# A two-layer hybrid trunk on one core: attention's first pairs inside the projections, a reordered last head step, six-chunk loads

## The chip, the core and the metric

The kernel runs on 1 core of one Trainium2 chip. The metric is the device time of one execution in microseconds (us), as the median of 3 runs. Engines are named as the profile names them: PE (TensorE), DVE (VectorE), ACT (ScalarE), POOL (GpSimd), SP (SyncE, which issues the loads).

## The reference, cut to what matters

Two layers run over 256 context and 512 latent tokens of width 1024, in float32. Layer 0 mixes tokens with a bidirectional gated recurrence (8 heads of 128), layer 1 with windowed attention. Each is followed by a feed-forward block with a 3x3 depthwise convolution. All of it is modulated by rows made from `c` and `ada_w`.

```python
def gla_chunk_step(state, q, v, k, g):            # layer 0, one chunk, both directions
    b = jnp.cumsum(g, axis=-2)
    o_inter = einsum(q * jnp.exp(b), state)
    o_intra = einsum(einsum(q, k, decay), v)
    state = jnp.exp(b_end)[..., :, None] * state + einsum(k * jnp.exp(b_end - b), v)
...
def sink_attend(q, keys, vals, sink, mask):       # layer 1, per block of 128 queries
    logits = where(mask, einsum('bqgrd,bkgd->bgrqk', q, keys) * 64 ** -0.5, -inf)
    m = maximum(max(logits, axis=-1), sink)
    p = exp(logits - m[..., None])
    o = einsum('bgrqk,bkgd->bqgrd', p / (sum(p, axis=-1) + exp(sink - m)), vals)
...
def conv_ffn(h, w_up, conv_w, conv_b, w_down, on_grid):
    u, v = split(h @ w_up)
    return (gelu(conv3x3(u) + conv_b) * v) @ w_down
```

## The kernel before, in words

**Matrix products.** Every activation and weight is split into a high and a low part (`HH`/`HL`, `WH`/`WL`), and each product is three matmuls. A weight tile is 8 chunks of 128x128 (512 KB). SP loads it into `WR[t % 3]` once tile t-3 is done (L387), ACT makes `WH` from it (`split_high`, L1106), DVE makes `WL` in the place of `WR` (`split_low`, L1555), and PE waits for that (`begin_tile`). ACT and DVE do this up to two tiles ahead of the tile that they follow, at fixed places of their instruction order. `depth(t)` says how many chunks are loaded and split: 6 for the eight tiles of the first output projection, 8 for all others. The third group of each feed-forward block has only 6 chunks of rows (`GROUPS = (8, 8, 6)`), so the last two chunks of its eight down tiles are zeros that PE never multiplies.

**The recurrence.** Each of the 8 heads has a step: seven levels of scores on PE (`level_scores`), between which DVE merges keys, queries and totals and takes the scores out of `MA` (`take`). PE does the next head's projections in between. The states of head h are made during the step of head h+1: PE turns the keys (`key_value`, L679), ACT copies them, PE multiplies them with the values (L687), DVE adds the states up (`states`, L1830 and L1832), and PE makes the outputs (`outputs`, L696). `key_value` waits for the final keys of the head (`kq_final`), for the modulation row (`ada_ready`, L1594), and for the scores to be taken (`scores_read`) before it writes `MA`. In steps 0 to 6 half a projection tile stands ahead of `key_value` on PE. In the last step (`last_head_step`) there is no projection left, PE begins with `key_value`, and fills the gaps with units of the output projection (`out_units`), one chunk of one tile each. Such a unit needs the low part of a finished head, which POOL makes (L409, `early_lo`) from ACT's high part.

**Attention.** Twelve tiles of projections come first (tiles `T_AT` to `T_AT + 11`), in two halves of key, four queries and value. DVE rotates keys and queries, ACT rounds them (L1459). Then 32 pairs of units (two heads, one block of 128 queries each) go round: PE makes a pair's scores into `MB` and `MA` (L933), DVE masks them and takes the maximum into `PB` (`masked_max`, L2159), ACT takes the exponential (`at_exp`, L1495), DVE inverts the sum (L2167), POOL scales (L440), PE turns the probabilities into `SLOT[0]` (L943), ACT copies them (L1509), and every four pairs PE multiplies with the values (L966). There is one `MB` and one `MA`: the scores of pair k wait for the maxima of pair k-1 (`row_max`). Scores run `LEAD = 2` pairs ahead of the turns. There are 7 buffers `PB`. The first three lie where the end of `HL` is (read until the last projection), the last four where the raw modulation weights were.

Of the kernel before, what the change touches and what calls it, by code (L numbers as in the profile page):

```python
# [27 lines left out]
P = 128  # L28
# [53 lines left out]

def depth(t):

    return EARLY if T_HGO <= t < T_HGO + KC else KC


# [23 lines left out]
def trunk(nc, small_in, x_in, ada_in, w_in, ident_in, masks_in, rope_in, rot_in, tri_in, out):  # L111
    ctx = ExitStack()
    with ctx:
# [3 lines left out]
        def sem(name):  # L117
            return ctx.enter_context(nc.semaphore(name))
# [13 lines left out]
        WH = [sb(f"WH{i}", [P, KC, P], F32R) for i in range(NB)]  # L132
        with ExitStack() as s:
            rope = sb("rope", [P, 2, LAT], F32, s)
            PB += [sb(f"PB{i}", [P, 5 * P + 1], F32, s) for i in range(3, 7)]
        AR0 = sb("ada_raw", [P, 4, 2, 512])
        AR = [AR0[:, i, :, :] for i in range(4)]
        ident = sb("ident", [P, P])
# [106 lines left out]
        level_ready, scores_done, scores_read = sem("level_ready"), sem("scores_done"), sem("scores_read")  # L245
        keys_ready, keys_mixed = sem("keys_ready"), sem("keys_mixed")
        v_turned, v_ready = sem("v_turned"), sem("v_ready")
        kq_final, k_turned, kt_ready = sem("kq_final"), sem("k_turned"), sem("kt_ready")
        kv_done, states_ready = sem("kv_done"), sem("states_ready")
        early_hi, early_lo = sem("early_hi"), sem("early_lo")  # L250
# [93 lines left out]
        def _(sp):  # L344
# [26 lines left out]
            def weights(t):  # L371

                if T_AT < t < T_AT + 6:
                    return w_in[T_AT - 2 + AT_ORDER[t - T_AT]]
                if T_FF0 < t < T_FF0 + 3:
                    return w_in[T_FF0 - 2 + (2 if t == T_FF0 + 1 else 1)]
                if t < T_HGO:
                    return w_in[t]
                if t < T_HGO + KC:
                    return w_in[t, :, 0:EARLY, :]  # L380
                if t < T_FF0:
                    return w_in[T_HGO:T_HGO + KC, :, t - KC - T_HGO + EARLY, :].rearrange("n p o -> p n o")
                return w_in[t - 2]

            for t in range(NB, STEPS):
                sp.wait_ge(tile_done, t - NB + 1)
# [16 lines left out]
        @block.gpsimd  # L403
        def _(pool):
            def split_heads():

                for h in range(HEADS - 1):
                    pool.wait_ge(early_hi, h + 1)
                    pool.tensor_tensor(HL[:, h, :], Y[:, h, :], HH[:, h, :].bitcast(F32), ALU.subtract).then_inc(early_lo, 1)  # L409

            def weights_low(t):

                pool.wait_ge(w_hi_done, t + 1)
                pool.wait_ge(w_split, t)
                pool.tensor_tensor(WL[t % NB][:, :, :], WR[t % NB][:, :, :], WH[t % NB][:, :, :].bitcast(F32), ALU.subtract).then_inc(w_split, 1)

            weights_low(0)
            split_heads()
            for t in POOL_LOWS:
                weights_low(t)  # L420

            def sink_columns():

                pool.wait_ge(nsink_ready, 1)
                for u in range(len(UNITS)):
                    i, bi, r, part = UNITS[u]
                    hd, n = i * 8 + part * 4 + r, chunks(u)
                    if u >= NPB:
                        pool.wait_ge(p_turned, u - NPB + 1)
                    pool.tensor_scalar(PB[u % NPB][:, n * P:n * P + 1], nsink[:, hd:hd + 1], 1.0, 0.0, ALU.mult, ALU.add).then_inc(sink_col, 1)  # L430
                    if u >= 3:
                        scaled_probs(u - 3)
                for u in range(len(UNITS) - 3, len(UNITS)):
                    scaled_probs(u)

            def scaled_probs(u):

                n = chunks(u) * P
                pool.wait_ge(rden_ready, u + 1)
                pool.tensor_scalar(PB[u % NPB][:, 0:n], PB[u % NPB][:, 0:n], rden[u % 4][:, :], 1.0, ALU.mult, ALU.mult).then_inc(probs_scaled, 1)  # L440

            pool.wait_ge(tile_done, T_AT + 12)
            sink_columns()

        @block.tensor
        def _(pe):
# [309 lines left out]
            def last_head_step(b):  # L756
# [4 lines left out]
                level_scores(b, -1)  # L761
                out_units(2)
                head_sums()
                level_scores(b, 0)
                out_units(7)
                level_scores(b, 1)
# [141 lines left out]
            def at_projections():  # L908

                first_tiles(TOK)  # L910
                third_tile(LAT)
                value_turns(MB, 1)
                for j in range(3):
                    full_tile((j + 1) % 2, LAT, HH, HL)
                full_tile(0, TOK, HH, HL)
                for j in range(4):
                    full_tile((j + 1) % 2, LAT, HH, HL)
                full_tile(1, TOK, HH, HL)

            def at_scores_of(k):  # L920

# [83 lines left out]
            def attention():  # L1005

                at_scores_of(0)
                pe.wait_ge(evacuated[0], tile.half(1))
                pe.wait_ge(evacuated[1], tile.half())
                value_turns(SLOT[0])  # L1010
                at_scores_of(1)
                pe.wait_ge(v_ready, vals.now(-2))
                for k in range(PAIRS):
                    if k + LEAD < PAIRS:
                        at_scores_of(k + LEAD)
                    at_turn(2 * k)
                    at_turn(2 * k + 1)
                    if k >= 4:
                        v, n = k // 4 - 1, chunks(8 * (k // 4 - 1))
                        cs = ((0, 1), (2, 3), (4,), ())[k % 4][:max(0, n - 2 * (k % 4))]  # L1020
# [73 lines left out]
        def _(act):  # L1094
# [377 lines left out]
            def projected(i):  # L1472
# [8 lines left out]
                for j in range(1, 5):  # L1481
                    raw((j + 1 - i) % 2, i * 6 + j)
                    rounded(i, j - 1)
                    if i == 0 and j == 1:
                        value_copy_at(0, MB)
                if i == 1:
                    new_values(i)
                rounded(i, 4)

            def at_exp(u):  # L1490

# [18 lines left out]

            def attention():

                at_exp(0)
                at_exp(1)
                value_copy_at(1, SLOT[0])
                for u in range(2, 2 * LEAD):
                    at_exp(u)
                for k in range(PAIRS):
                    at_copy(2 * k)
                    at_copy(2 * k + 1)  # L1520
                    for u in range(2 * k + 2 * LEAD, min(2 * k + 2 * LEAD + 2, len(UNITS))):
                        at_exp(u)
                    if k in EARLY_OUT:
# [14 lines left out]
        def _(dve):  # L1538
# [312 lines left out]
            def head_step(b, parity, h, j0, tail=True, project=True):  # L1851
# [12 lines left out]
                for n in range(LEVELS):  # L1864
                    merge_keys(b, n)
                    if tail and n == 0:
                        head_out(h - 1)
                    merge_queries(b, n, taken.now() + 1)
                    take(n)
                    merge_totals(b, n)  # L1870
                    if project and n in (0, 2, 3, 4):
                        split_low(first + (3 if n == 0 else n + 2))
                rows.add()
                ada_add(j0)
                if project:
                    gate(parity, h + 1)

# [8 lines left out]
            def last_head_step(b, j0):  # L1886

                forget(b, 0, 7)
                decayed_queries(b)
                states(1 - b)  # L1890
                diagonal(b)
                head.add()
                take(LEVELS)
                split_low(T_HGO + 2)
# [235 lines left out]
            def projected(i):  # L2130
# [7 lines left out]
                rope_low(5 * i)  # L2138
                for j in range(1, 5):
                    rope_sums(5 * i + j)  # L2140
                    split_low(first + j + 3)
                    rope_low(5 * i + j)
                tile.add(6)
# [44 lines left out]

            def attention():

                for u in range(2 * LEAD):
                    masked_max(u)
                    if u >= 2:
                        inverse_sum(u - 2)
                for k in range(PAIRS):
                    for u in range(2 * k + 2 * LEAD, min(2 * k + 2 * LEAD + 2, len(UNITS))):
                        masked_max(u)
# [124 lines left out]
```

## Time and profile before

| | us |
|---|---|
| median of 3 runs | 1839.48 (1839.29 to 1841.08) |
| the profiled execution's own time | 1840.51 |
| its span in the profile | 1838.4 |
| PE busy | 1795.9 (98%) |
| DVE busy | 1163.5 (63%) |
| ACT busy | 680.5 (37%) |
| POOL busy | 79.3 (4%) |
| head steps and first projections, 60 to 600: PE busy of 540.0 | 532.9 |
| attention pairs, 1289 to 1403: PE busy of 114.0 | 103.2 |
| end of the last feed-forward and final norm, 1784 to 1838.4: PE busy of 54.4 | 44.2 |

The profiled execution's own time is its span and 2.1 us around it. Its rows give times from the start of the span. The granted PE clock is given as a share of 2.4 GHz: 1.00 is full speed and 0.50 is 1.2 GHz.

### The profile page before, as it was taken

Reading aid. Unit: us, or ns where it says so; the run is one execution under the profiler, and the core shown is the slowest. Engines: PE = TensorE matmul, PEld = TensorE weight load, DVE = VectorE, ACT = ScalarE, POOL = GpSimd, SP = SyncE. Lnnn points to the kernel's source line nnn. Section 1 sums busy time; section 2 is a strip of 40 time slices with the busy share of each in tenths; the row PEclk is TensorE's granted clock in tenths of the full one; section 3 lists DMA queues with packets and bytes.
Section 4 is the critical chain, followed back from the end, with each engine's and each line's share of the span. In section 5 each row is a group of like instructions: output and inputs, shape, how many; then the busy total and the mean of one; then the engine's idle time right before and its main releaser. Section 6 shows DMA issues by size and latency. Waiting matters only on the chain.

```text
span 1838.4 us, 31654 instructions
## 1 busy us (share of the span) xinstructions
PE 1795.9 (98%) x13574; PEld 1535.3 (84%) x13574; DVE 1163.5 (63%) x1934; ACT 680.5 (37%) x1009; POOL 79.3 (4%) x142
## 2 busy tenths in 40 slices
PE   8999999999999999999999999999899999999997
PEld 7999999999888788888888888888556888888886
DVE  5366668666887776425653356477555697487585
ACT  4334434443432433213331132343775343243233
POOL 0000000000110100000000000000453000000000
PEclk9999999999999999999999999999999999999998
DMA  9321222112211233223323232222000232232233
GB/s 307 106 102 41 88 93 93 67 65 90 85 45 35 81 115 115 94 108 120 115 92 104 104 123 92 84 71 83 12 1 24 69 106 100 93 99 96 92 102 105
DMA packets 54154, 166.18 MB, mean 90 GB/s; under 512 B 5120, under 2 KB 15744, under 8 KB 54016
## 3 DMA queue, kind: packets, MB, share of 16 engines
q1 hardware_dynamic: 54016, 164.16, 26.0%
q8 instruction: 108, 1.77, 0.4%
q14 instruction: 30, 0.25, 0.0%
HBM read 162.05 MB, written 2.10 MB: 89 GB/s over the span
## 4 chain that ended last, share of the span: by engine, by line
PE 91%; DVE 5%; ACT 2%; issue 1%; DMA 1%; POOL 0%; DVEq 0%; SPq 0%; ACTq 0%
PE slot L478 31%; PE slot L466 8%; PE slot L468 7%; PE slot L467 7%; PE slot L1051 4%; PE slot L1053 4%; PE slot L1052 4%; PE MA L662 2%; PE MB L535 2%; PE MA L1051 2%; PE MA L1053 2%; PE MA L1052 2%; PE slot L966 2%; PE MB L933 1%; PE slot L943 1%
## 5 line engine op out<-in xcount | busy, mean ns | idle before, releaser
L1555 DVE TENSOR_TENSOR WL<-WR,WH 128x1024 fp32r<-128x1024 f32 (+1 forms) x203 | 246.0, 1212 | 206.4 <-ACT WH L1106 204.8
L1106 ACT ACTIVATE WH<-WR 128x1024 fp32r<-128x1024 f32 (+1 forms) x206 | 215.9, 1048 | 381.1 <-DMA WR<-in_w 381.1
L466 PE MATMUL slot<-HH,WH 128*128 128x384 f32 (+2 forms) x768 | 270.7, 353 | 9.7 <-DVE HL L1656 5.0
L468 PE MATMUL slot<-HH,WL 128*128 128x384 f32 (+2 forms) x768 | 261.6, 341 | 0.0
L467 PE MATMUL slot<-HL,WH 128*128 128x384 f32 (+2 forms) x768 | 261.5, 340 | 0.0
L478 PE MATMUL slot<-HH,WH 128*128 128x256 f32 (+1 forms) x768 | 201.9, 345 | 0.3 <-DVE WL L1555 0.3
L478 PE MATMUL slot<-HH,WL 128*128 128x256 f32 (+1 forms) x768 | 198.5, 340 | 0.0
L478 PE MATMUL slot<-HL,WH 128*128 128x256 f32 (+1 forms) x768 | 196.0, 337 | 0.0
L466 PEld LDWEIGHTS slot<-HH,WH 128*128 128x128 f32 x768 | 145.0, 189 | 23.8 <-DVE HL L1656 6.0
L478 PEld LDWEIGHTS slot<-HH,WH 128*128 128x128 f32 x768 | 141.5, 189 | 23.9 <-issue 5.7
L478 PEld LDWEIGHTS slot<-HL,WH 128*128 128x128 f32 x768 | 145.0, 189 | 17.1
L478 PEld LDWEIGHTS slot<-HH,WL 128*128 128x128 f32 x768 | 144.7, 188 | 16.5
L468 PEld LDWEIGHTS slot<-HH,WL 128*128 128x128 f32 x768 | 144.7, 188 | 4.1
L467 PEld LDWEIGHTS slot<-HL,WH 128*128 128x128 f32 x768 | 144.9, 189 | 3.2
L2064 DVE SCALAR_TENSOR_TENSOR ACC<-UP,cw,ACC 128x512 f32<-128x512 f32 x176 | 132.0, 750 | 20.9 <-ACT ACC L1413 17.7
L1992 DVE SCALAR_TENSOR_TENSOR ACC<-UP,cw,ACC 128x512 f32<-128x512 f32 x176 | 131.9, 750 | 3.9
L1051 PE MATMUL slot<-HH,WH 128*128 128x512 f32 x256 | 99.9, 390 | 0.0
L1052 PE MATMUL slot<-HL,WH 128*128 128x512 f32 x256 | 99.6, 389 | 0.0
L1053 PE MATMUL slot<-HH,WL 128*128 128x512 f32 x256 | 99.6, 389 | 0.0
L478 PE MATMUL slot<-GH,WH 128*128 128x256 f32 (+1 forms) x308 | 79.0, 338 | 0.0
L478 PE MATMUL slot<-GL,WH 128*128 128x256 f32 (+1 forms) x308 | 78.4, 336 | 0.0
L478 PE MATMUL slot<-GH,WL 128*128 128x256 f32 (+1 forms) x308 | 78.4, 335 | 0.0
(297 smaller groups left out, 3167.7 us busy)
## 6 DMA issues: line engine op xcount, KB each, us to landing
WR<-in_w SPq DMA_DIRECT2D x198, 512.0 KB, 3.5
ada_raw<-in_ada SPq DMA_DIRECT2D x84, 512.0 KB, 4.5
AD<-in_ada SPq DMA_DIRECT2D x12, 512.0 KB, 8.5
X<-in_x SPq DMA_DIRECT2D x4, 768.0 KB, 9.1
WR<-in_w SPq DMA_DIRECT2D x8, 384.0 KB, 3.0
out<-Y SPq DMA_DIRECT2D x8, 256.0 KB, 2.2
Y<-in_masks SPq DMA_DIRECT2D x1, 512.0 KB, 8.8
rope<-in_rope SPq DMA_DIRECT2D x1, 512.0 KB, 3.8
```

The lines of the kernel that those rows point to most:

```text
L466: mm(SLOT[s][:, po], WH[w % NB][:, k, :], hi[:, k, to], start=(k == 0), stop=False)
L467: mm(SLOT[s][:, po], WH[w % NB][:, k, :], lo[:, k, to], start=False, stop=False)
L468: last = mm(SLOT[s][:, po], WL[w % NB][:, k, :], hi[:, k, to], start=False, stop=(k == kn - 1))
L478: last = mm(dst[:, po], wt[w % NB][:, k, :], x[:, k, to], start=(k == 0 and part == 0), stop=(k == kn - 1 and part == 2))
L535: last = mm(MB[32 * m:32 * m + 32, 0:P], silu_w[:, c, :], src(f)[:, m * P:(m + 1) * P], start=(c == 0), stop=(c == KC - 1))
L1051: mm(dst, WH[w % NB][:, k, :], hi[:, k, t], start=(k == 0), stop=False)
L1052: mm(dst, WH[w % NB][:, k, :], lo[:, k, t], start=False, stop=False)
L1053: last = mm(dst, WL[w % NB][:, k, :], hi[:, k, t], start=False, stop=(k == kn - 1))
L1106: go(WH[t % NB][:, 0:depth(t), :], WR[t % NB][:, 0:depth(t), :], ACT.Copy).then_inc(w_hi_done, 1)
L1555: tt(WL[t % NB][:, 0:k, :], WR[t % NB][:, 0:k, :], WH[t % NB][:, 0:k, :].bitcast(F32), ALU.subtract).then_inc(w_split, 1)
L1992: ins = stt(acc, lat[:, dy:dy + GRID_H, dx:dx + GRID_W], cw[b][:, k:k + 1], acc, ALU.mult, ALU.add)
L2064: ins = stt(acc, grid[:, dy:dy + GRID_H, dx:dx + GRID_W], cw[b][:, k:k + 1], acc, ALU.mult, ALU.add)
```

## The change

It has three parts.

1. **Attention's first pairs.** The four `PB` buffers in the modulation weights' place now come first in the ring. PE makes the scores of pair 0 ahead of the last projection tile, those of pair 1 inside it (after 5 of its 8 chunks), and those of pair 2 right behind it. The maxima, exponentials and the first inverse sum of units 0 to 3 move into the projections' code on DVE and ACT, between the rotation and rounding of the last query and the copy of the last values. POOL starts its sink columns once tile `T_AT + 6` is done, and waits for the last tile ahead of unit 4. The turn of the last values on PE moves behind the turns of units 0 and 1, and goes to `SLOT[1]`.
2. **Head steps.** In every head step but the last, DVE adds the modulation row ahead of the last `take` and the last totals, and no longer behind them. In the last head's step DVE makes the states and the diagonal first and the decayed queries behind them; a new semaphore `queries_ready` holds PE's `level_scores(b, 0)` until then.
3. **Six chunks.** `depth(t)` is 6 for the last eight tiles of both feed-forward blocks, for the load and both splits.

```diff
 def depth(t):
 
+    if T_AT - KC <= t < T_AT or t >= STEPS - KC:
+        return GROUPS[-1]
     return EARLY if T_HGO <= t < T_HGO + KC else KC
...
-            PB += [sb(f"PB{i}", [P, 5 * P + 1], F32, s) for i in range(3, 7)]
+            PB = [sb(f"PB{i}", [P, 5 * P + 1], F32, s) for i in range(3, 7)] + PB
...
-                return w_in[t - 2]
+                return w_in[t - 2, :, 0:depth(t), :]
...
+                    if u == 2 * LEAD:
+                        pool.wait_ge(tile_done, T_AT + 12)
...
-            pool.wait_ge(tile_done, T_AT + 12)
+            pool.wait_ge(tile_done, T_AT + 7)
             sink_columns()
...
                 head_sums()
+                pe.wait_ge(queries_ready, 1)
                 level_scores(b, 0)
...
-                full_tile(1, TOK, HH, HL)
+
+            def at_last_tile():
+
+                begin_tile(1)
+                for k in range(KC):
+                    both_halves(1, k, HH, HL)
+                    if k == 4:
+                        at_scores_of(1)
...
                 at_scores_of(0)
+                at_last_tile()
+                at_scores_of(LEAD)
                 pe.wait_ge(evacuated[0], tile.half(1))
-                pe.wait_ge(evacuated[1], tile.half())
-                value_turns(SLOT[0])
-                at_scores_of(1)
-                pe.wait_ge(v_ready, vals.now(-2))
                 for k in range(PAIRS):
-                    if k + LEAD < PAIRS:
+                    if 0 < k < PAIRS - LEAD:
                         at_scores_of(k + LEAD)
                     at_turn(2 * k)
                     at_turn(2 * k + 1)
+                    if k == 0:
+                        pe.wait_ge(evacuated[1], tile.half())
+                        value_turns(SLOT[1])
+                    if k == 3:
+                        pe.wait_ge(v_ready, vals.now(-2))
...
                     rounded(i, j - 1)
+                    if i == 1 and j == 4:
+                        at_exp(0)
+                        at_exp(1)
+                        rounded(i, 4)
+                        at_exp(2)
+                        at_exp(3)
...
                 if i == 1:
                     new_values(i)
-                rounded(i, 4)
+                else:
+                    rounded(i, 4)
...
-                at_exp(0)
-                at_exp(1)
-                value_copy_at(1, SLOT[0])
-                for u in range(2, 2 * LEAD):
-                    at_exp(u)
                 for k in range(PAIRS):
                     at_copy(2 * k)
                     at_copy(2 * k + 1)
+                    if k == 0:
+                        value_copy_at(1, SLOT[1])
...
                     merge_queries(b, n, taken.now() + 1)
+                    if n == LEVELS - 1:
+                        rows.add()
+                        ada_add(j0)
                     take(n)
...
-                rows.add()
-                ada_add(j0)
...
                 forget(b, 0, 7)
-                decayed_queries(b)
                 states(1 - b)
                 diagonal(b)
+                tt(QQ[b][:, :, :], Q[:, :].unsqueeze(1).to_broadcast([P, 2, TOK]), FD[b][:, :, :], ALU.mult).then_inc(queries_ready, 1)
...
                     rope_sums(5 * i + j)
+                    if i == 1 and j == 4:
+                        masked_max(0)
+                        masked_max(1)
+                        inverse_sum(0)
+                        rope_low(5 * i + j)
+                        masked_max(2)
+                        inverse_sum(1)
+                        masked_max(3)
+                        split_low(first + j + 3)
+                        continue
                     split_low(first + j + 3)
                     rope_low(5 * i + j)
...
-                for u in range(2 * LEAD):
-                    masked_max(u)
-                    if u >= 2:
-                        inverse_sum(u - 2)
```

## Rows read from the trace of the kernel before

**Rows 1.** Waits of PE, 1500:1838: us in total, times, longest.

```profile
PE slot L1051 <- DVE WL L1555: 1.0, 1, 1.0
...
PE slot L1051 <- DVE GL L2039: 0.5, 1, 0.5
```

**Rows 2.** Chain that ended last, the last projection tile: start, us.

```profile
1280.76 8.49 PE slot L478 x48
```

**Rows 3.** PE timeline, start of attention: start us, us, [idle before <-releaser].

```profile
1289.16 0.38 PE L933 MATMUL MB<-KH,QH 64*128 64x256 f32 x1
...
1290.32 0.85 PE L905 MATMUL slot<-ident,AVT 128*128 128x128 f32 x6 [0.17 <-ACT AVT L1470]
1292.90 0.35 PE L933 MATMUL MB<-KH,QH 64*128 64x256 f32 x1 [1.74 <-DVE nmax L2159]
...
1295.56 0.55 PE L933 MATMUL MB<-KH,QH 64*128 64x256 f32 x1 [1.68 <-DVE nmax L2159]
...
1298.84 0.38 PE L933 MATMUL MB<-KH,QH 64*128 64x256 f32 x1
```

**Rows 4.** DVE timeline, last tile and start of attention.

```profile
1284.76 0.69 DVE L2121 TENSOR_TENSOR RAW<-RAW,ROT 128x512 f32<-128x512 f32 x1
...
1291.33 0.74 DVE L2159 CUSTOM_DVE_ANT_0 PB<-MB,edge,nsink 128x512 f32<-128x512 f32 x1
```

**Rows 5.** ACT timeline, the same stretch.

```profile
1289.27 0.90 ACT L1470 ACTIVATE AVT<-slot,small 128x768 f32<-128x768 f32 x1 [3.95 <-PE slot L478]
...
1292.12 0.72 ACT L1495 ACTIVATE PB<-PB,nmax 128x513 f32<-128x513 f32 x1
```

**Rows 6.** PE timeline, into the last head's step.

```profile
495.20 0.33 PE L528 MATMUL MB<-ident,RB 128*128 128x128 f32 x1
499.20 0.90 PE L679 MATMUL MB<-ident,KK 128*128 128x128 f32 x6 [3.68 <-issue]
...
508.60 0.38 PE L696 MATMUL MB<-PS,V 128*128 128x128 f32 x2
...
515.16 0.27 PE L662 MATMUL MA<-QQ,KL 128*32 128x32 f32 x4
```

**Rows 7.** DVE timeline, into the last head's step.

```profile
496.26 1.04 DVE L1817 COPY_PREDICATED PS<-masks,MA 128x384 f32<-128x384 uint8 x2
497.20 1.83 DVE L1805 TENSOR_TENSOR FD<-FD 128x6 f32<-128x6 f32 x2
498.95 0.15 DVE L1594 TENSOR_TENSOR ada<-MB,small 128x8 f32<-128x8 f32 x1
...
501.56 1.76 DVE L1764 TENSOR_TENSOR QQ<-Q,FD 128x1536 f32<-128x1536 f32 x1
504.57 0.29 DVE L1830 COPY SF<-MB 128x128 f32<-128x128 f32 x1 [1.25 <-PE MB L687]
...
508.04 1.39 DVE L1769 TENSOR_TENSOR KL<-KK 128x768 f32<-128x768 f32 x1
```

**Rows 8.** POOL timeline, the same stretch.

```profile
497.11 3.60 POOL L409 TENSOR_TENSOR HL<-Y,HH 128x768 fp32r<-128x768 f32 x2 [471.97 <-ACT HH L1237]
```

**Rows 9.** One stretch: us, busy us and count of PE, PEld, DVE, ACT, POOL, clock, DMA.

```profile
500.00:503.00 3.00, 3.00 (x13) 2.81 (x12) 2.97 (x2) 2.39 (x4) 0.71 (x1) 0.50 0.02 7
```

**Rows 10.** The page's DMA issues: count, KB each, us to landing.

```profile
WR<-in_w SPq DMA_DIRECT2D x198, 512.0 KB, 3.5
...
WR<-in_w SPq DMA_DIRECT2D x8, 384.0 KB, 3.0
```

**Rows 11.** Groups by shape, weight splits, DVE then ACT: count | busy us, mean ns.

```profile
L1555 DVE TENSOR_TENSOR WL<-WR,WH 128x1024 fp32r<-128x1024 f32 x195 | 238.4, 1223 | 205.1 <-ACT WH L1106 203.5 <-DVE KO L2135 0.3
...
L1555 DVE TENSOR_TENSOR WL<-WR,WH 128x768 fp32r<-128x768 f32 x8 | 7.6, 952 | 1.3 <-ACT WH L1106 1.3
...
L1106 ACT ACTIVATE WH<-WR 128x1024 fp32r<-128x1024 f32 x198 | 209.2, 1057 | 375.3 <-DMA WR<-in_w 375.3
...
L1106 ACT ACTIVATE WH<-WR 128x768 fp32r<-128x768 f32 x8 | 6.7, 836 | 5.9 <-DMA WR<-in_w 5.9
```

More of the change, by code:

```diff
@@ L247, in trunk @@
         v_turned, v_ready = sem("v_turned"), sem("v_ready")
+        queries_ready = sem("queries_ready")
         kq_final, k_turned, kt_ready = sem("kq_final"), sem("k_turned"), sem("kt_ready")
```

## The prediction

> **What bounds the kernel now.** I read the page first: PE is busy 98% of the span, so time can only come out of PE's idle gaps or its slow clock. The list of PE's waits says where the gaps are, the timelines of each gap say which chain ends it. Three gaps matter here. At the start of attention PE stops for 1.74 us and 1.68 us, each time for a maximum from DVE, and the next scores run at half clock (0.55 us for the form that takes 0.38 us before and after) [rows 3]. At the start of the last head's step it stops for 3.68 us [rows 6], and then runs 3.0 us at clock 0.50 [rows 9]. In the last feed-forward it stops for 0.5 us for a `GL` chunk and for 1.0 us for a `WL` tile [rows 1]. The reader is to see in each what the awaited engine was doing just before: it was doing other work, or its chain started late.
>
> **Attention's start.** PE's order before is last tile, scores 0, value turns, scores 1, scores 2, turns of pair 0, scores 3. The last tile runs 1280.76 to 1289.16, 8.40 us [rows 2, 3]; scores of a pair take 0.95 us (1289.16 to 1290.15, where the 0.17 us wait before the turns begins) [rows 3]. A pair's maxima hold the next scores for 1.57 us from DVE's first maximum (1291.33 to 1292.90) [rows 3, 4].
>
> Afterwards, step by step. Scores 0 put the last tile at 1281.7. Its fifth chunk ends 5/8 of 8.40 later, 1286.95. DVE ends the last query's rotation at 1285.45 [rows 4], so the maxima of pair 0 start at 1285.4 and release PE at 1287.0, which costs 0.05. Scores 1 end at 1287.95, the tile's other three chunks (3.15) at T = 1291.1. On ACT an exponential starts 0.79 after its maximum (1291.33 to 1292.12) and takes 0.72 [rows 4, 5]: units 0 and 1 run from 1286.2 to 1287.6. The last rounding and DVE's low part behind it are passes over 512 columns as long as the rotation's (0.69) [rows 4], less overlap 1.3 together: 1288.9. The maxima of units 2 and 3 start there and release PE at about 1288.9 + 1.65 = 1290.55 (1.57 and a small inverse between), ahead of T. So scores 2 follow the tile without a gap and end at 1292.05.
>
> What is late next is ACT. Its fourth exponential ends at 1291.15; then comes `WH` of tile T_AT+13 (1.06) [rows 11], which before was hidden inside the last tile, and only then the copy of the last values (0.90) [rows 5], ready at 1293.0. DVE's `split_low` of that tile waits for it from 1290.4 to 1292.25 and takes 1.15 net, and the maxima of units 4 and 5 are queued behind it: 1293.4, PE released at 1293.4 + 1.57 = 1295.0. Meanwhile PE turns units 0 and 1 and the values: 8 and 6 turns, six of which take 0.85 [rows 3], so about 2.0 us, to 1294.1. POOL's scaling of unit 1 is held until T and lies under scores 2; uncovered, it would eat into the 0.9 us that PE then stops for the maxima anyway. So scores 3 start at 1295.0 where they started at 1298.84 [rows 3]: **3.85 us**. From there the order, the buffers and the lead of two pairs are those of before, each pair again held by the one `MB` and `MA`, so the 3.85 stay. The moved matmuls are the same in number; the removed gaps are 3.6 and the lost half clock about 1.1, less a new gap of about 0.9. Bounds: 4.8 if DVE's stop for the `WH` copy (0.9 of PE's time) costs nothing, 2.0 if ACT's block is late by two exponentials and a copy more and PE stops at T for it.
>
> **The last head's step.** PE has its row turned at 495.53 and then needs the add. DVE does it at 498.95, behind a `take` (from 496.26) and the totals (1.83 us for two operations on 6 columns) [rows 6, 7]. The queries' merge before the `take` is over at 496.26. With the add there (0.15), `ada_ready` comes at 496.4 and `key_value` starts at 496.55 in place of 499.20: 2.65 us. Its `MA` half waits for the `take` (1.04), which then ends at 497.45: six turns (0.65) behind 496.55, PE stops for 0.25. The first unit of the output projection needs POOL's first low part, which ends at 497.11 + 1.81 (half of 3.60) = 498.95, PE would be there at 497.45 + 0.65 = 498.1: with the signal's way, 0.95 lost [rows 8]. Between 499.20 and 508.60 PE had no other gap, and 3.0 us of that were at half clock, worth 1.5 [rows 6, 9]. With the gap cut from 3.68 to 1.0 I take it that the clock holds: outputs could start at 508.60 - 2.65 + 0.25 + 0.95 - 1.5 = 505.65. The states must be there. DVE's sequence up to the forget product ends at 501.56 as before (the add only changed places, `take` and totals are still in it). The states took 3.47 (504.57 to 508.04) [rows 7]; ahead of the queries they run from 501.6, when the first products arrive, to 505.1. With the queries' product (1.76) still in front they would end at 506.9 and cost PE 1.25. So outputs start at 505.65 against 508.60: **2.95 us**. Bounds: 1.45 if the clock falls again, 3.5 if PE doesn't meet the two short waits' full lengths.
>
> The product then runs behind the diagonal. Queued behind it on DVE are the first `take` and the split of tile T_HGO+2. Its reader is `level_scores(b, 0)`, 6.55 us behind the start of outputs (508.60 to 515.16) [rows 6]: 512.2. Diagonal and product cost 1.39 and 1.76 [rows 7] behind 505.1, so 508.25, a cover of 3.95 us; POOL has four other low parts to make, 1.8 each [rows 8], and each of the two may stand behind one of them, so at the latest 511.9, still covered. In steps 0 to 5 PE has half a projection tile ahead of `key_value`, and shows no stop there: the earlier add is worth nothing.
>
> Here a rule bears on the move. DVE's totals, both inputs in SBUF, took 1.83 for 6 columns and ended at 499.03, just as POOL's first low part was over (498.9) [rows 7, 8]. The Trainium skill (SBUF — State Buffer, the practical consequences of the shared port pair) says that a DVE instruction with two SBUF inputs and a GpSimd instruction that reads SBUF exclude each other, the second waiting until the first has finished. By that rule the queries' product, which ran alone before, can be held by POOL for whole operations. The trace agrees in that one place. By rule or by row, the sum stays, because of the cover above; the case where the hold is longer than the cover is a rival below.
>
> **Six chunks.** `WH` falls from 1.06 to 0.84, `WL` from 1.22 to 0.95 [rows 11], a load from 3.5 to 3.0 [rows 10]. The first gap (0.5) ends a chain of ACT and DVE work that has one `WH` and one `WL` of a down tile in it: 0.22 + 0.27 = 0.49 off, the gap is gone. The second (1.0) is the fourth down tile, loaded only when the first is done: load, `WH` and `WL` in series, 0.5 + 0.22 + 0.27 = 0.99 off, gone too. **1.45 us**. In layer 0's block PE waits nowhere in these tiles, so nothing there. Bounds: 0.5 (the load lands no earlier) to 1.5 (both gaps are all there is).
>
> **Sum.** 3.85 + 2.95 + 1.45 = 8.25. The profiled execution took 1840.51 (span 1838.4 and 2.1 around it), so 1832.25; the median lies 1.03 below that execution, so 1831.2, 0.45% less.
>
> **Rivals.**
> - *The clock falls again in the last head's step.* For it: in about 3.5 us PE still stops for 1.0, 0.25 and 0.95, and at attention's start it fell with no gap above 1.74 [rows 3]. Against: the longest gap is a third of before. The step gives 1.45, time 1832.7. Chance 0.2.
> - *ACT's block is late.* Exponentials, rounding, `WH` and value copy in one queue delay the first pairs' turns; attention gives 2.0, time 1833.1. Chance 0.13.
> - *The queries' product is held by POOL beyond its cover.* At 511.9 plus the first `take` (1.04) PE waits 0.7, and one POOL operation more makes it 2.5: time 1833.7. Chance 0.07.
> - *The six chunks do nothing*, since ACT's table load and not the load decides when `WH` starts: 1832.2 to 1832.7, inside the range. Chance 0.08.
> - *Slower: PE stays at half clock in attention's pairs.* Scores, turns and short stops alternate there, and it did fall for three microseconds at their start. A microsecond of work at 2.4 GHz costs one more at 1.2, so from 8.25 us of work more at the low clock the gain is gone, and from 12 on it is over 0.2% slower. With 20, the time is about 1843. Against it: the gaps get fewer, and the same pairs kept full speed before. Chance 0.03.
>
> **How the numbers follow.** The forecast has 0.49. A measurement of this kernel can tell about 0.2% (3.7 us) from no change, so faster means below 1835.8. The rivals above zero gain reach 1833.7 one at a time, two together 1835; the best case (4.8 + 3.5 + 1.5) gives 1829.7. The range 1829.0 to 1835.0 leaves out the slow side, three rivals together and gains beyond all three bounds: under 2 in 10. Faster 0.92, same 0.05, slower 0.03.
>
> **What would show it.** Right: the last tile with scores 1 inside and no stop over 0.2 us; scores 2 right behind it; a stop near 0.9 ahead of scores 3 that is DVE's maximum; L1594 ahead of the last `take`; the stop before L679 near 1.0 and none before L696; no wait for `WL` or `GL` at the end. Wrong: a stop in the middle of the last tile, a clock of 0.50 in the last head's step or over a long stretch of attention, a new wait at L662 for `QQ`, or pair cycles that are longer than before.

## The result, and the profile of the changed kernel

The changed kernel takes 1829.49 us (median, 1828.4 to 1830.8) where the kernel before took 1839.51 beside it: ratio 0.9942, 95% interval 0.9928 to 0.9955. It is faster by 10.0 us by the medians and 10.7 by the ratio, where 8.25 was forecast. The forecast time was 1831.2, with a range down to 1829.0: the median of 1829.49 lies at that end of it, and the ratio applied to 1839.48 gives 1828.8, past it. The same file measured again on another chip gave 1831.47 and 0.9955 (0.9942 to 0.9967), 8.1 to 8.3 us. Two single executions of the experiments at a far lower granted clock, 2331 us of the kernel before (0.70) and 2508 us of the one with six chunks alone (0.65), are left out of the ratios.

The profiled execution took 1828.88 us, its span is 1826.7 against 1838.4. To place the 11.7 us between the spans, I measured the distance from one landmark on PE to the next in both traces. The start of the kernel, which no line of the change touches, is 1.60 shorter. The last head's step is 3.04 shorter (forecast 2.95), the stretch from the norm ahead of attention's projections to the fifth scores 4.00 (forecast 3.85; counted from the end of the last query tile alone it is 4.05), the end of the last feed-forward 1.27 (forecast 1.45). What is left is 0.24 in the norms and first feed-forward, 0.60 in the norm behind attention and 0.95 around the final norm. So the three parts sum to 8.31 where 8.25 was forecast, and 3.4 us come from places that the prediction didn't count. The other head steps, in which the add also moved, took the same: 341.45 and 341.46 us from the first head's sums to the last head's row turn, as forecast.

**Attention's start.** PE's timeline; it answers to [rows 3].

```profile
1275.79 0.38 PE L946 MATMUL MB<-KH,QH 64*128 64x256 f32 x1
...
1282.11 0.38 PE L946 MATMUL MB<-KH,QH 64*128 64x256 f32 x1
...
1286.34 0.38 PE L946 MATMUL MB<-KH,QH 64*128 64x256 f32 x1
...
1287.25 1.09 PE L956 MATMUL slot<-ident,PB 128*128 128x128 f32 x8
1288.18 0.82 PE L911 MATMUL slot<-ident,AVT 128*128 128x128 f32 x6
1289.97 0.35 PE L946 MATMUL MB<-KH,QH 64*128 64x256 f32 x1 [0.98 <-DVE nmax L2190]
...
1292.57 0.35 PE L946 MATMUL MB<-KH,QH 64*128 64x256 f32 x1 [0.34 <-DVE nmax L2190]
```

These are the first matmuls of scores 0 to 4, with two groups of turns ahead of scores 3. Scores 0, 1 and 2 have no bracket (a bracket is idle time of the engine, and what ended it): the two stops of 1.74 and 1.68 us are gone, and each scores' first matmul takes 0.38, so the clock is full. One new stop of 0.98 stands ahead of scores 3. What ends it is seen on ACT, then on DVE, in the same stretch:

```profile
1286.19 1.04 ACT L1122 ACTIVATE WH<-WR 128x1024 fp32r<-128x1024 f32 x1
1287.13 0.88 ACT L1486 ACTIVATE AVT<-slot,small 128x768 f32<-128x768 f32 x1
```

```profile
1287.26 1.23 DVE L1575 TENSOR_TENSOR WL<-WR,WH 128x1024 fp32r<-128x1024 f32 x1 [1.83 <-ACT WH L1122]
1288.40 0.74 DVE L2190 CUSTOM_DVE_ANT_0 PB<-MB,edge,nsink 128x512 f32<-128x512 f32 x1
```

DVE is idle for 1.83 us until ACT's `WH` copy, makes `WL`, and only then starts the maximum of unit 4, whose data had been there since 1287.2. This is the chain that the prediction named.

**The last head's step.** PE's timeline, which answers to [rows 6], and one stretch of it with its clock, which answers to [rows 9].

```profile
493.62 0.33 PE L533 MATMUL MB<-ident,RB 128*128 128x128 f32 x1
494.94 0.85 PE L684 MATMUL MB<-ident,KK 128*128 128x128 f32 x6 [0.99 <-DVE QQ L1810]
495.87 0.87 PE L684 MATMUL MA<-ident,KK 128*128 128x128 f32 x6
497.50 0.59 PE L483 MATMUL slot<-HH,WH 128*128 128x256 f32 x2 [0.76 <-POOL HL L412]
...
503.98 0.38 PE L701 MATMUL MB<-PS,V 128*128 128x128 f32 x2
...
510.51 0.27 PE L667 MATMUL MA<-QQ,KL 128*32 128x32 f32 x4
```

```profile
500.00:503.00 3.00, 3.00 (x23) 2.75 (x22) 2.66 (x10) 1.25 (x2) 3.00 (x2) 1.00 0.00 0
```

The stop of 3.68 is now 0.99, the clock stays at 1.00, and the outputs (L701) start 10.36 us behind the row turn (L533) instead of 13.40 (508.60 less 495.20). DVE in the same stretch, which answers to [rows 7]:

```profile
494.68 0.16 DVE L1614 TENSOR_TENSOR ada<-MB,small 128x8 f32<-128x8 f32 x1
494.75 1.05 DVE L1837 COPY_PREDICATED PS<-masks,MA 128x384 f32<-128x384 uint8 x2
495.70 1.76 DVE L1825 TENSOR_TENSOR FD<-FD 128x6 f32<-128x6 f32 x2
...
503.57 2.52 DVE L1789 TENSOR_TENSOR KL<-KK 128x768 f32<-128x768 f32 x1
506.02 3.36 DVE L1912 TENSOR_TENSOR QQ<-Q,FD 128x1536 f32<-128x1536 f32 x1
```

The queries' product took 3.36 where it took 1.76 alone, and the diagonal in front of it 2.52. The product ends at 509.38 and the `take` behind it at 510.35; PE comes for both at 510.51, without a stop, 0.16 to spare.

**The end.** PE's waits from 1500 on; they answer to [rows 1]:

```profile
PE MB L604 <- DVE rstd L1635: 0.6, 1, 0.6
PE slot L1067 <- DVE WL L1575: 0.2, 1, 0.2
```

Of the 1.5 us of stops in the down tiles 0.2 is left (0.5 in the second profile of this kernel). The wait for `rstd` is in the final norm, and is 0.6 in the kernel before too.

### The profile page after: what moved, and what is told of

It reads as the page before. It is cut to its first block, busy times and chain, and to the rows that moved or that the text cites. A ratio compares the mean times of both kernels' runs of the same rounds, so it can differ in the third digit from the quotient of the medians.

```text
span 1826.7 us, 31654 instructions
## 1 busy us (share of the span) xinstructions
PE 1791.4 (98%) x13574; PEld 1531.4 (84%) x13574; DVE 1160.4 (64%) x1934; ACT 677.0 (37%) x1009; POOL 81.0 (4%) x142
## 4 chain that ended last, share of the span: by engine, by line
PE 90%; DVE 6%; ACT 2%; issue 1%; DMA 1%; POOL 0%; DVEq 0%; SPq 0%
PE slot L483 30%; PE slot L471 8%; PE slot L473 7%; PE slot L472 7%; PE slot L1067 4%; PE slot L1069 4%; PE slot L1068 4%; PE MA L667 2%; PE MB L540 2%; PE MA L1069 2%; PE MA L1067 2%; PE MA L1068 2%; PE slot L979 2%; PE MB L946 1%; PE slot L956 1%
## 5 line engine op out<-in xcount | busy, mean ns | idle before, releaser
L1575 DVE TENSOR_TENSOR WL<-WR,WH 128x1024 fp32r<-128x1024 f32 (+1 forms) x203 | 241.8, 1192 | 202.8 <-ACT WH L1122 201.5
```

What stands on the lines that cost most here:

```text
L1575: tt(WL[t % NB][:, 0:k, :], WR[t % NB][:, 0:k, :], WH[t % NB][:, 0:k, :].bitcast(F32), ALU.subtract).then_inc(w_split, 1)
```

## The experiments

Ratios are to the kernel before, run on the same chip. "Outputs" is the distance from the last row turn to the first matmul of the outputs; by it a run's luck at the start drops out. Each run has one profiled execution. Two theories were to be told apart. The first: the three parts give what the prediction's sum says, and the rest of the 10.0 us is the spread of single runs. The second: one part brings more than it was priced at.

**The kernel before once more**

> The kernel before once more, unchanged, for a second profile of it. The changed kernel's profiled span is 11.7 us shorter, of which the three changed places hold 3.90 (attention's start), 2.99 (last head's step) and 1.28 (last down tiles), 8.17 together; the other 3.5 lie where no line was changed: 1.6 before 130 us, 0.4 around the first feed-forward's norm, 0.6 at the norm behind attention and 0.9 at the final norm. Theory 1, these are one run's luck (when the first loads land, and whether PE's clock is at half there): the second profile of before shows other values in these places, by up to 2 us in sum, and the same values in the changed places within 0.1. Theory 2, they belong to the kernel before: the second profile shows the same clock of 0.50 behind 1828 and 0.66 from 1455 to 1460, and a time within 0.3 us of 1839.5.

1840.35 us, span 1838.2. Neither theory held whole. Of the places without changed lines, the norm behind attention moved as luck would have it: 6.77 us from its first sum to the next product where the first profile has 8.47, and no low clock there; the start didn't move. But a changed place moved too, by 0.8 and not within 0.1: outputs came 14.21 us behind the row turn, not 13.40. The clock in the stretch was low for 6.8 us, not 3.4.

**Each part alone**

First attention's part (the last tile with scores 1 inside, the scores, maxima and exponentials moved, POOL's earlier start), then the head steps' part, then the loads:

```
 def depth(t):
+    if T_AT - KC <= t < T_AT or t >= STEPS - KC:
+        return GROUPS[-1]
...
-                return w_in[t - 2]
+                return w_in[t - 2, :, 0:depth(t), :]
```

> Attention's part alone. Theory 1 (the places add up, each with its own size): 3.9 us less than before, ratio 0.9979, plus up to 1.5 if the norm behind attention keeps its clock. Theory 2 (the parts help one another through PE's clock): about a third of the 10 us, but not 3.9. In the trace scores 3 start 3.9 us sooner than in before, counted from the end of the last query tile; the half clock at scores 2 is gone.

> The head steps' part alone. Theory 1: 3.0 us less than before, ratio 0.9984. In the trace the outputs start 10.4 us behind the turned row (13.4 in before), with stops of 1.0 and 0.8 us ahead of them. Theory 2: the earlier phase changes the clock at the first norm as well, up to 1 us more.

> The six-chunk part alone. Theory 1: 1.3 to 1.5 us less than before, ratio 0.9992, all of it in the last eight tiles, none in layer 0. Theory 2: PE's clock at the final norm fell because of the two stops of 0.5 and 1.0 us ahead of it; then the clock behind 1826 stays full as well and the part is worth 2.2 us.

| part alone | us | ratio (95%) | gain in us, from the ratio |
|---|---|---|---|
| attention's start | 1836.81 | 0.9977 (0.9968 to 0.9986) | 4.2 |
| last head's step | 1837.50 | 0.9979 (0.9969 to 0.9988) | 3.9 |
| six chunks | 1837.85 | 0.9986 (0.9977 to 0.9995) | 2.6 |

Each interval is about 1.7 us to either side, so the sum, 10.7, is good to some 3 us (the three added as independent errors). The traces are finer. From the end of the last query tile to the fifth scores attention's kernel took 16.77 us, and the changed kernel 16.78 and 16.77 in its two profiles. The nine profiles in which this place is as before fall into two groups: 20.8 to 21.0 in five of them, both of the kernel before among these, and 21.7 in four, where the clock was low for 6.8 us and not 3.4. One of the four is the kernel with the states' move alone, below:

```profile
1292.00:1298.00 6.00, 4.32 (x30) 3.58 (x27) 3.13 (x12) 3.18 (x8) 1.77 (x5) 0.50 0.00 0
```

So this part gives 4.05 to 4.9 us. In the head's kernel outputs came at 10.37, with the stops 0.99 and 0.75. In the kernel with six chunks all waits for `WL` and `GL` were gone; its outputs came at 14.16, again later than 13.40. The measured sum agrees with the whole gain, and of the two theories the second has the head's step and attention's start on its side: both are priced against an execution with a short stretch of low clock, and often it is longer.

**The changed kernel again, and two mended versions**

The second kernel puts ACT's `WH` copy ahead of the third exponential; the third one also gives PE its `key_value` whole, ahead of the first projection unit.

```
                         at_exp(1)
+                        split_high(tile.now() + AHEAD)
                         rounded(i, 4)
...
-                key_value(1 - b, 1)
-                out_units(3)
+                key_value(1 - b)
+                out_units(4)
```

> The changed kernel once more, unchanged, beside the same runs of before as the next ones. Before itself spread over 1836.2 to 1845.1 in 26 runs. Theory 1 (the changed places give 8.2 by the one profile, and a little more on average since before's half clock in the last head's step was 3.0 us long in its first profile and 5 to 6 us in three others): 8.9 to 9.5 us less than before, ratio 0.995. Theory 2 (a further gain somewhere else): 10 us or more, ratio at or below 0.9945, and a stretch without changed lines that is shorter than in all profiles of before.

> The changed kernel with ACT's high part of weight tile T_AT+13 moved ahead of the exponentials of units 2 and 3, where ACT stood idle for 1.43 us. Theory 1 (the stop of 0.98 ahead of scores 3 is DVE waiting for that copy, with the maxima of units 4 and 5 queued behind it): the stop goes, scores 3 start 0.9 to 1.0 sooner, and so does all that follows; 0.9 us less than the changed kernel. Theory 2 (the exponentials are late by it, or POOL's scaling is next): the stop shrinks by less than 0.5, the time is the same.

> As the one before, and in the last head's step PE multiplies keys and values ahead of the first output unit and makes four units behind them in place of one and three. Theory 1 (PE's stop of 0.76 is POOL's first low part; the key copies of ACT are ready sooner): the outputs start 0.3 to 0.5 sooner than in the changed kernel, so 1.3 us less than it in all. Theory 2 (then the states end the wait): a stop of 0.3 to 0.5 ahead of the outputs takes its place and nothing is won.

The changed kernel: 1831.47, ratio 0.9955, 8.1 to 8.3 us and so less than the 8.9 to 9.5 that I expected. With the early `WH`: 1830.47, 0.9948 (0.9935 to 0.9960). With both: 1830.05, 0.9949 (0.9935 to 0.9962). The times can't tell the three apart, but the traces do. With the early `WH` the stop ahead of scores 3 is gone and scores 3 start 13.14 us behind scores 0 (1278.11 there), not 14.18:

```profile
1291.25 0.37 PE L946 MATMUL MB<-KH,QH 64*128 64x256 f32 x1
```

This shows that the copy's place was what made the stop. With `key_value` whole outputs came at 10.06, as PE now waits for 0.20 in place of 0.76:

```profile
495.15 0.85 PE L684 MATMUL MB<-ident,KK 128*128 128x128 f32 x6 [0.99 <-DVE QQ L1811]
497.15 1.38 PE L692 MATMUL MB<-V,RF 128*128 128x128 f32 x10 [0.20 <-ACT RF L1243]
```

**The early add alone, and the states' move alone**

The early add is in the kernel before, with the product still in front of the states:

```
+                    if n == LEVELS - 1:
+                        rows.add()
+                        ada_add(j0)
                     take(n)
...
-                rows.add()
-                ada_add(j0)
```

> Before with the earlier modulation row alone. Theory 1: the stop ahead of the key turns falls from 3.68 to 1.0 and the clock stays full; the outputs then wait for the states, which the queries' product holds 1.2 to 1.8 longer: outputs start 11.6 to 12.2 us behind the turned row (13.4 to 14.3 in before, 10.36 in the changed kernel). Theory 2 (the clock still falls at the shorter stop): 13 us or more.

1839.89 us, ratio 1.0004 (0.9994 to 1.0013): nothing. I had expected outputs at 12.2 at the most; they came at 13.34. The stop before the key turns did fall to 0.99, and the clock held, but DVE and PE show where it went:

```profile
500.33 3.28 DVE L1764 TENSOR_TENSOR QQ<-Q,FD 128x1536 f32<-128x1536 f32 x1
503.64 0.29 DVE L1830 COPY SF<-MB 128x128 f32<-128x128 f32 x1
```

```profile
507.25 0.49 PE L696 MATMUL MB<-PS,V 128*128 128x128 f32 x2 [2.81 <-DVE SB L1832]
```

The product takes 3.28 in place of 1.76, the states behind it are late, and PE stops for 2.81 ahead of the outputs. POOL's timeline has its third and fourth low parts there:

```profile
499.43 2.56 POOL L409 TENSOR_TENSOR HL<-Y,HH 128x768 fp32r<-128x768 f32 x1
501.95 3.34 POOL L409 TENSOR_TENSOR HL<-Y,HH 128x768 fp32r<-128x768 f32 x1
```

The third ends at 501.99, the product 1.62 later, and the fourth low part 1.68 after the product: each in turn, about as long as it takes alone.

The other half, with the add where it was:

```
                 forget(b, 0, 7)
-                decayed_queries(b)
                 states(1 - b)
                 diagonal(b)
+                tt(QQ[b][:, :, :], Q[:, :].unsqueeze(1).to_broadcast([P, 2, TOK]), FD[b][:, :, :], ALU.mult).then_inc(queries_ready, 1)
```

> The kernel before, with the states and the diagonal put ahead of the queries' product and a signal for its reader; the add of the modulation row stays where it was. Theory 1 (in the kernel before, the late add alone sets the last head's step, and the states are not the last thing that PE waits for): the stop of 3.68 us before the key turns stays, the clock still falls behind it, outputs start 13.4 to 14.4 us behind the row turn as before, and the time is that of before within 0.5 us. Theory 2 (the states are what counts): outputs start 12.5 us or less behind the row turn, and 1 us or more is won although the stop stays.

1840.85, ratio 1.0006 (0.9997 to 1.0016); outputs at 14.25, the stop 3.67. So neither move brings anything alone, and both together bring 3 to 4 us: each takes away a limit behind which the other one stands. The clock in the head's step of this kernel (columns as in [rows 9]):

```profile
495.00:497.00 2.00, 0.00 (x0) 0.00 (x0) 2.00 (x5) 1.97 (x4) 0.68 (x1) 0.94 0.91 352
497.00:499.00 2.00, 0.59 (x3) 0.63 (x4) 2.00 (x4) 0.00 (x0) 2.00 (x2) 0.50 0.87 342
499.00:503.00 4.00, 4.00 (x18) 3.71 (x17) 1.73 (x2) 2.58 (x4) 1.06 (x2) 0.50 0.02 6
503.00:504.00 1.00, 1.00 (x8) 1.00 (x7) 0.00 (x0) 1.00 (x2) 1.00 (x1) 0.72 0.00 0
```

Here the clock fell to 0.50 (1.2 GHz) while PE still stood, and the key turns began at 498.40 at the low clock. In the profile shown ahead of the prediction the turns began at 499.20 at the full clock, and it fell 0.7 us later:

```profile
499.00:500.00 1.00, 0.80 (x7) 0.83 (x8) 1.00 (x4) 0.00 (x0) 1.00 (x1) 0.93 0.52 209
```

**What held the product**

Both kernels above have POOL's low parts beside DVE. This one is the kernel with the early add alone, in which POOL waits for the product ahead of its third low part:

```
+                    if h == 2:
+                        pool.wait_ge(queries_ready, 1)
```

> The kernel before with the early add alone, and with POOL made to wait ahead of its third low part until DVE has made the queries' product, which stays in its old place ahead of the states. With the early add alone the product took 3.28 us in place of 1.76, and outputs came 13.34 us behind the row turn. Theory 1 (POOL's low part held the product, and the product's length is what ate the add's gain): the product takes 1.75 us again, the stop before the outputs falls from 2.81 to 1.3 us, outputs start 11.8 us behind the row turn, and the time is 1.5 us below that of before. Rival (something else lengthened it, or PE waits for the states whatever the product takes): the product stays above 2.5 us, or outputs stay at 13.0 us or later.

DVE, then PE:

```profile
500.11 1.76 DVE L1894 TENSOR_TENSOR QQ<-Q,FD 128x1536 f32<-128x1536 f32 x1
501.79 0.28 DVE L1834 COPY SF<-MB 128x128 f32<-128x128 f32 x1
```

```profile
505.39 0.49 PE L699 MATMUL MB<-PS,V 128*128 128x128 f32 x2 [1.16 <-DVE SB L1836]
```

The product is back at 1.76, the stop falls from 2.81 to 1.16, outputs come at 11.68 in place of 13.34: the expected sizes. 1838.94 us, ratio 0.9994 (0.9985 to 1.0003): below the kernel before by 1.1 us, in the expected direction, though the interval doesn't exclude nothing. So POOL's low part is what held the product. The Trainium skill (SBUF — State Buffer, Who interferes with whom, practical consequences) says that a DVE instruction with two SBUF inputs contends with a GpSimd instruction that reads SBUF; the runs agree, with 1.5 to 1.6 us for one hold.

**The price of the half clock**

The kernel before, with idle matmuls in the 3.68 us stop and nothing else changed, first with 14 and then with 8 of them:

```
             def last_head_step(b):

+                pe.wait_ge(evacuated[0], tile.half(1))
+                keep_busy(8, SLOT[0][:, 512:768])
                 key_value(1 - b, 1)
```

> The kernel before, with idle matmuls put into the 3.68 us stop of the last head's step: no work is taken away or moved, and PE still starts the key turns when the add is ready. It measures the price of the half clock behind the stop alone. Theory 1 (the stop is what drops the clock, and the half clock costs what half of its 3.0 us comes to): the granted clock stays near 1.00, outputs start 11.9 us behind the row turn in place of 13.40, 1.5 us won. Theory 2 (the profile shown was the mild case, as in three repeats outputs came 14.15 to 14.35 us behind the row turn): outputs at 11.9 and 2.2 to 2.5 us won in time. Rival: the clock falls in the same place whether PE idles or not; outputs stay at 13.4 or later and nothing is won.

> As the kernel before with idle matmuls in the stop of the last head's step, but 8 in place of 14: the 14 ran 6.21 us, 2 us beyond the add, and ate what the clock gave back. 8 run about 3.6 us and end at the add. Theory (the stop drops the clock, and the half clock costs 1.67 us in the profile shown and 2.52 us in another, as the stretch from the first key turn to the outputs was 9.40 and 10.25 us there and 7.73 us with the clock held): the clock stays at 1.00, the key turns start 4.0 us and outputs 11.6 to 11.8 us behind the row turn, in place of 13.40 to 14.35, and the time is 1.7 to 2.5 us below that of before. Rival (with PE faster, something else becomes last, such as the states behind the queries' product): a wait for DVE's states shows ahead of the outputs, and less than 1 us is won.

The 14 ran for 6.21 us, 2 us beyond the add (I had counted them as half as long), so outputs came at 13.94 and the time didn't move: 1840.24, ratio 1.0001 (0.9993 to 1.0010). But the clock was 1.00 throughout, and from the first key turn to the outputs it took 7.73 us. With 8, PE's timeline and its clock (columns as in [rows 9]):

```profile
495.59 3.62 PE L605 MATMUL slot<-small,ident 128*128 128x256 f32 x16
499.45 0.85 PE L679 MATMUL MB<-ident,KK 128*128 128x128 f32 x6 [0.24 <-issue]
...
507.22 0.49 PE L696 MATMUL MB<-PS,V 128*128 128x128 f32 x2
```

```profile
499.00:500.00 1.00, 0.76 (x6) 1.00 0.70 287
500.00:501.00 1.00, 1.00 (x11) 1.00 0.08 16
```

(In this answer only PE's busy time stands before the clock.) Outputs at 11.79, from the first key turn 7.77. The same stretch took 9.40 in the profile of before [rows 6], so its half clock cost about 1.65; in the kernel with the states moved it took 10.25, a cost of 2.5. In time: 1839.67 beside 1841.09, ratio 0.9992 (0.9983 to 1.0001), 1.5 us less by the ratio, where I expected 1.7 to 2.5; the interval's upper end is no change, so that the gain in time isn't shown. The trace does show that the stop is what drops the clock: with PE busy in it, and no work taken away, the clock stayed at 1.00 in both profiles, where it fell in all five with the stop left idle.

## Where the prediction was right, and which step of it failed

The direction, the places and the new stops were right. The time was 1.7 us too high for the first measurement (2.4 by its ratio), which lies at or past the end of the range, and 0.3 too low for the second.

**The step that failed is the price of the half clock**, "3.0 us of that were at half clock, worth 1.5" in the last head's step and "the lost half clock about 1.1" at attention's start, each sized on one execution.

- **Last head's step, 2.95: 3.04 against the profile shown, 3.9 against the usual one.** Key turns came 2.68 earlier (2.65 forecast), the `take` stop was about 0.25 (0.25), POOL's 0.76 (0.95). The clock held, as the forecast took it. The 1.5 is right for the execution shown (1.65 measured), and not for most. In the five profiles that leave this step as it was, or move the states only, outputs came at 13.40, 14.21, 14.35, 14.16 and 14.25: the execution I read was the mild one, with the clock low for 3.4 us and not 6.8. Against the mean of the other four, 14.24, the step is worth 3.9.
- **Attention, 3.85: 4.05 against the profile shown, 4.5 on average.** From scores 2 to scores 3 it took 3.28 us before (1295.56 to 1298.84, [rows 3]); scores and as many turns take 1.84 at the full clock (1286.34 to 1288.18), so that the half clock cost 1.44 and not 1.1. In the four profiles with a longer low clock the start took 0.7 to 0.9 more. Against the mean of the nine profiles, 21.3, the 16.78 of the changed kernel is 4.5 less. The new stop was to be about 0.9 and is 0.98, for ACT's `WH` copy, and moving that copy removes it. "ACT's block is late" (2.0) didn't come: ACT's fourth exponential was over at 1286.2, before the tile's end at 1286.3.
- **Six chunks, 1.45: measured 1.27**, as one wait of 0.2 for `WL` is left in the changed kernel; in the other three profiles with all parts the wait is 0.4 to 0.5, and 1.0 to 1.1 is won. In the kernel with this part alone none is left, and the same stretch is shorter by 1.56 (39.54 against 41.10). One profile without this part, the head steps' kernel, has a stop of 1.8 there in place of 1.0 and a lower clock behind it, and takes 2.4 us longer than the kernel before.

The three parts come to about 9.5 us so (4.5, 3.9 and 1.1) in place of 8.25. The two measurements, 10.7 and 8.3 by their ratios, lie to either side of it.

**The range had a second fault: all that lies outside the three parts was put at nothing.** Its best case, 1829.7, is the three upper bounds and no more, and one measurement passed it. In the first pair of profiles the rest came to 3.4 us, 1.60 at the start and 1.8 around the norms. The runs show this as the spread of single executions, no effect of the change:

- The row turn of one early step came at 131.7 and at 132.9 us in the two profiles of the changed kernel, and anywhere from 131.7 to 133.7 in the kernels of the experiments, all with the same code up to there.
- From the final norm's first sum to the end it took 12.88 us in the kernel before and 11.98 in the changed one. But two kernels without the six chunks, the head steps' and the one in which POOL waits, took 11.99 and 12.00, and the one with both mends 12.41.
- The norm behind attention took 8.47 and 6.69. Without any change of attention there are 6.77 (the kernel before itself), 6.78, 6.79 and 6.82, and with all of it 8.20 and 9.83. The clock fell there in the long ones and not in the short ones.

**The product in front: 1.25 in the text, 2.81 measured.** With POOL made to wait it was 1.16, so the sum was right for the product at its length alone (1.76); the hold by POOL, which I had in the next paragraph, was left out. It did no harm to the forecast, since the change moves the product, but it was the reason for my miss on the early add alone. The rival of a hold beyond the cover had a chance of 0.07; the hold came in full (3.36, and 2.52 for the diagonal), and the cover held by 0.16 us. I would give it more now.

What stays open is the last microsecond: whether the gain is 8.3 or 10.7 can't be told from these runs. Both intervals hold 8.3 to 10.7, and the parts' sum in the traces (about 9.5) lies there. Nor is it shown why the low clock lasts 3.4 us in one execution and 6.8 in the next. No version ran that is measurably better than the changed kernel; its trace with both mends is better by 1.3 us in the two places that they touch.

## What to carry to other kernels

A stop behind which the clock falls costs its own length and a variable fee after it: read that stretch in several executions before you price it, and ask whether idle matmuls in the stop bring the clock's share at once (here the trace showed it, the time only 1.5 us with an interval that touches no change). Give the range a term for the places that the change doesn't touch. When two late things stand one behind the other (an add that starts PE, and states that feed its outputs), test them together: each alone may measure as nothing. Give a DVE pass with two SBUF inputs that is moved beside a POOL pass one POOL operation more than its own length, and look whether its reader still comes later.

## What the runs showed of the hardware

- One and the same stop of 3.68 us was followed by the half clock at different times: from 0.7 us after PE went on [rows 6, 9], or from inside the stop (the kernel with the states moved, low at 497 and until past 503). The difference was 0.85 us in that step. Stops of 0.99 and 0.76 left it at 1.00 in all six profiles that have both.
- Short stops can bring the half clock too. At attention's start PE never stood longer than 1.74 us at a time, and the clock fell in all nine profiles with the two stops; in the kernel with the states moved it was at 0.50 from 1292 on, behind the first of them.
- A hold by POOL lengthened a 1536-column product from 1.76 to 3.28 and 3.36 us, and a 768-column pass to 2.52; POOL's own passes, 1.80 to 1.87 mostly, took up to 3.34. In the kernel in which POOL waited for the product, that product took 1.76 again.
- The kernel before spread from 1836.2 to 1845.1 us over 26 runs on one chip, 9 us, as much as the change is worth. One profile can stand 0.8 us off the others in a single step.
